# Hybrid decoder step: every third key unit multiplied on GpSimd instead of VectorE

## The chip, the cores and the metric

The kernel runs on one core of a Trainium2 chip, as one launch. Times are device microseconds. The engines are TensorE (PE, matrix products), VectorE (DVE), ScalarE (ACT), GpSimd (POOL) and SyncE (SP, which here only issues transfers). Each engine works through its own list of instructions in order; semaphores tie the lists together. What is measured is the time of one execution, as the median of several; less is better.

## The reference, cut to what matters

One inference step of a two-layer decoder trunk runs for a prompt of 1024 tokens and for 8 single new tokens (samples). The first layer has two groups of heads side by side: stick-breaking attention and an RWKV-7 recurrence. Each sample attends with 8 heads of 64 columns over 8192 old keys and values, which lie in pages of 128 tokens, 64 pages a sample, in an order given by a page table. The part that this change touches is the scores of the samples against the old keys:

```python
z = einsum('bthd,bshd->bhts', q, past_k) * DH_A ** -0.5 + bias      # one query row a sample
w = sb_weights(z, ...)                                             # sums over later positions
o = einsum('bhts,bshd->bthd', w, past_v)
```

The recurrence of the prompt, which runs at the same time in the kernel, is computed in 8 pairs of chunks of 64 tokens, each pair by gram matrices, a triangular solve in five levels, and an update of the state.

## The kernel before, in words

The kernel is a row of phases with a barrier between them. Sample work on pages is spread over four of them (the projections of values and of RWKV inputs, the prompt's attention, and the recurrent stage `rwkv_phase`) by a class `Pages`, whose methods add instructions to the list of each engine at the places where the phases call them.

A key unit is two key pages: 128 tokens on the partitions, 2 x 512 columns. There are 256 units, 32 a sample. SyncE loads the pages into a ring of 8 pages, that is 4 units (`load_keys`, L1018 reads the page number, L1019 issues the transfer), each after the semaphore `k_used` says that its slot is free. `keys_dve` handles a unit on VectorE in two instructions: L1108 multiplies the two pages by the query row, which has been copied to all partitions, into a buffer `prod`, and then frees the slots; L1111 sums groups of 64 columns of `prod` into 16 scores. The units 0 to 81 are done before the recurrent stage, by VectorE, and stay there.

In the recurrent stage a loop over `i` makes eight turns. VectorE's list of a turn is the recurrence of pair `i`, with `more(n)` between its steps, which puts `n` key units of sample `i + 1` there: 3, 2, 1, 2, 2, 1, 2, 2, 2, 2 and at the end 6, 25 in all. (The last turn has none; it puts the steps of the sample state there.) In this document the units of a turn are counted 0 to 24. After the last one `bias_dve` (L1125) adds the bias, and ScalarE (L1077 to L1079) and VectorE (L1130) start on the softplus of that sample at the head of the next turn. L2120, L2127, L2140 and L2143 are the masked copies of the solve; the first `L2033` with `rw_dh` is the update of the state, which waits for TensorE.

GpSimd issues the transfers of the value pages, which are weighted and added by TensorE (L1048, four pages a group, twelve groups of the current sample and four of the one before in a turn). The ring of value pages has 12 slots, so page `at` waits until page `at - 12` has been used; the page number is read into a register first (`load_values`, L1070). Before the first page of each sample GpSimd issues the next pair's input rows (`rows`, L1481), which ScalarE reads (L1811) in the next turn. Pages of a sample are counted 0 to 63 here; a sample's pages 0 to 47 are used in its own turn, 48 to 63 in the next.

Before the stage GpSimd clears small buffers (L1483 to L1485); nothing else of its work is arithmetic.

Of the kernel before, what the change touches and what calls it, by code (L numbers as in the profile page):

```python
# [17 lines left out]
ALU = mybir.AluOpType  # L18
ACT = mybir.ActivationFunctionType
AX = mybir.AxisListType  # L20

P = 128
D_MODEL = 1024
SEQ = 1024
NS = 8
# [4 lines left out]
H_A, DH = 8, 64  # L30
D_A = H_A * DH
PAST, PAGE = 8192, 128
NPG = PAST // PAGE
# [10 lines left out]
NPAIR = SEQ // (2 * C)  # L44
# [65 lines left out]
class Sems:  # L110


    def __init__(self, nc, phase):
        self.nc, self.phase, self.all = nc, phase, []
# [841 lines left out]
class Pages:  # L956
# [3 lines left out]
    RING = 8  # L960
    VRING = 12
    ZRING = 4
    UNITS = NPG // 2

    def __init__(self, T, ctx):
        nc = T.nc
        self.T, self.nc = T, nc
        self.sems = sems = Sems(nc, "pages")
        self.k_in = [sems(f"k_in{n}") for n in range(self.RING)]
        self.v_in = [sems(f"v_in{n}") for n in range(self.VRING)]  # L970
        (self.qc_in, self.q_turned, self.q_copied, self.q_stored, self.q_in, self.table_in, self.k_used, self.v_used,
         self.reduced, self.biased, self.logged, self.softplus_ready, self.summed, self.z_ready, self.w_ready,
         self.cleared, self.folded, self.selected, self.picked, self.step, self.act_step) = (
            sems(n) for n in ("qc_in", "q_turned", "q_copied", "q_stored", "q_in", "table_in", "k_used", "v_used",
                              "reduced", "biased", "logged", "softplus_ready", "summed", "z_ready", "w_ready",
                              "fold_cleared", "folded", "selected", "picked", "page_step", "page_act_step"))
        sb = lambda n, s, d=F32: ctx.enter_context(nc.sbuf_tensor("pg" + n, s, d))
        self.kp = sb("_k", [P, self.RING, D_A])
        self.qc, self.q = sb("_qc", [P, 4, NS]), sb("_q", [P, 2, D_A])
        self.fold = sb("_fold", [P, D_A])  # L980
        self.qr = self.fold[0:NS, :]
        self.prod = sb("_prod", [P, 2, D_A])
        self.z = sb("_z", [P, self.ZRING, H_A, NPG])
        self.zb, self.sp = sb("_zb", [P, H_A * NPG]), sb("_sp", [P, H_A * NPG])
        self.wts = sb("_w", [P, 2, H_A * NPG])
        self.table = sb("_table", [1, NS * NPG], I32)
        self.q_rows = nc.dram_tensor("scratch_pg_q", [NS, D_A], F32, kind="Internal").ap()
        self.fetched, self.unit = 0, 0
# [71 lines left out]
    def start_act(self, act):  # L1060
        act.wait_ge(self.cleared, 1)
        act.wait_ge(self.q_turned, 1)
        act.activation(self.qr, self.T.ps[0:NS, 7, :], ACT.Copy, scale=DH ** -0.5).then_inc(self.q_copied, 1)

    def load_values(self, pool, pages):

        for at in pages:
            pool.wait_ge(self.v_used, at + 1)
            page = pool.value_load(self.table[0:1, at:at + 1], min_val=0, max_val=self.T.n_phys - 1)
            pool.dma_start(self.vp[:, at % self.VRING, :], self.T.io["v_pages"][bass.ds(page, 1), :, :]  # L1070
                           .rearrange("a p n -> (a p) n")).then_inc(self.v_in[at % self.VRING], 16)
# [27 lines left out]
    def keys_dve(self, dve, n):  # L1099

        for u in range(self.unit, min(self.unit + n, NS * self.UNITS)):
            b, g, at = u // self.UNITS, 2 * u % NPG, 2 * u % self.RING
            if g == 0:
                dve.wait_ge(self.q_in, 16 * b + 16)
            for e in range(2):
                dve.wait_ge(self.k_in[at + e], 16 * (2 * u // self.RING) + 16)
            dve.wait_ge(self.reduced, u + 1)
            dve.tensor_tensor(self.prod[:, :, :], self.kp[:, at:at + 2, :],  # L1108
                              self.q[:, b % 2, :].unsqueeze(1).to_broadcast([P, 2, D_A]), ALU.mult).then_inc(self.k_used, 2)
            dve.wait_ge(self.k_used, self.RING + 2 * u + 2)  # L1110
            dve.tensor_reduce(self.z[:, b % self.ZRING, :, g:g + 2].rearrange("p h n -> p n h"),  # L1111
                              self.prod[:, :, :].rearrange("p n (h d) -> p n h d", h=H_A), AX.X, ALU.add)\
               .then_inc(self.reduced, 1)
            self.unit = u + 1

# [4 lines left out]
    def bias_dve(self, dve, b):  # L1120
        assert self.unit >= self.UNITS * (b + 1)
        dve.wait_ge(self.reduced, self.UNITS * (b + 1) + 1)
        if b:
            dve.wait_ge(self.w_ready, b)
        dve.tensor_tensor(self.zb[:, :].rearrange("p (h n) -> p h n", h=H_A), self.z[:, b % self.ZRING, :, :],  # L1125
                          self.T.vec("sb_bias").unsqueeze(2).to_broadcast([P, H_A, NPG]), ALU.add).then_inc(self.biased, 1)
# [14 lines left out]


KEYS_V, KEYS_PB, KEYS_ATT, KEYS_TURN = 16, 42, 24, 25


def attention_phase(T):
# [239 lines left out]
def rwkv_phase(T):  # L1386
# [6 lines left out]
    nc, h, ps, io = T.nc, T.h, T.ps, T.io  # L1393
    sems = Sems(nc, "rwkv")
# [14 lines left out]
    pages = T.pages  # L1409
    with ExitStack() as ctx:  # L1410
# [23 lines left out]
        u, r0 = ur[:, 0, :], ur[:, 1, :]  # L1434
# [25 lines left out]
        def _(sp):  # L1460
            pages.load_keys(sp, NS * Pages.UNITS)
            sp.wait_ge(pages.k_used, Pages.RING + NS * NPG)
# [13 lines left out]
        @block.gpsimd  # L1476
        def _(pool):
            def rows(i):
                pool.wait_ge(S["turned"], i)
                pool.wait_ge(S["bonus_used"], prep(i - 1) + 1)  # L1480
                pool.dma_start(X[:, :, :], xs[:, :, i * W:(i + 1) * W]).then_inc(xs_in, 16)  # L1481

            pool.memset(main["eg"][:, :, :], 1.0)  # L1483
            pool.memset(smpl["eg"][:, :, :], 1.0)
            pool.memset(Hx[:, :, :, :], 0.0).then_inc(S["cleared"], 1)  # L1485
            pool.wait_ge(S["cleared"], 1)
            pool.sem_inc(S["h_ready"], 1)
            done = Pages.VRING
            for i in range(1, NPAIR):
                rows(i)  # L1490
                pages.load_values(pool, range(done, NPG * i))
                done = NPG * i
            pages.load_values(pool, range(done, NPG * NS))

        @block.tensor
        def _(pe):
# [1705 lines left out]
```

## Time and profile before

| | us |
|---|---|
| timed runs, median of 3 (lowest to highest) | 4689.95 (4687.75 to 4692.08) |
| profiled execution, its own time | 4680.17 |
| its span, first to last instruction | 4678.6 |
| TensorE busy in the span | 3857.8 |
| VectorE busy | 2356.5 |
| ScalarE busy | 1174.9 |
| GpSimd busy | 401.3 |
| key units on VectorE, multiplies (L1108, 256 times) | 313.5 |
| key units on VectorE, sums (L1111, 256 times) | 312.9 |
| value page issues on GpSimd (L1070, 512 times) | 276.3 |

The recurrent stage lies at about 694 to 1540 us of the span. A busy time is the time in which an engine had an instruction at work; waits on semaphores, register work and the issuing of transfers by SyncE are not counted. In the rows further down, "start us, us" is when an instruction or a merged row of them began and how long it took; "x2" counts them; a bracket gives the idle time of the engine just before and what ended it. "<-issue" is idle time for which the profile shows no other engine.

### The profile page before, as it was taken

The numbers are of one execution on the slowest core, as the hardware profiler recorded it, in microseconds if no ns is written. First come the engines' busy times: TensorE is split into PE (matmuls) and PEld (weight loads), VectorE is DVE, ScalarE is ACT, GpSimd is POOL, SyncE is SP. The second block draws the span as 40 slices with busy tenths as digits, with TensorE's granted clock in tenths as the row PEclk, the third lists the DMA queues.
The fourth block names the chain that finished last, engine by engine and source line by source line (L and its number), as shares of the span: only waits on it lengthen the run. The fifth ranks groups of instructions, "written<-read, shape, count | busy, mean of one in ns | idle before, by whom it ended". The sixth has DMA issues, their size and how long they took to land. (4 is left out here: it accounts for less than half of the span.)

```text
span 4678.6 us, 77751 instructions
## 1 busy us (share of the span) xinstructions
PE 3857.8 (82%) x29645; PEld 3332.9 (71%) x29645; DVE 2356.5 (50%) x3054; ACT 1174.9 (25%) x1872; POOL 401.3 (9%) x739
## 2 busy tenths in 40 slices
PE   6887885676677769999896999788898187999999
PEld 5786333344444659999896888677777087999899
DVE  2488888888887224444312444444443524444511
ACT  3213662222222222222212222222221012222300
POOL 0011102333333100000000000000000000000000
PEclk8998997788888689999998999877777598999999
DMA  2465316988887321111122222210100231111122
GB/s 89 152 209 167 114 48 213 309 290 290 288 289 246 106 113 46 45 46 45 60 73 105 70 86 83 82 33 19 37 19 15 76 133 52 51 45 46 44 82 64
DMA packets 212106, 512.43 MB, mean 110 GB/s; under 512 B 34153, under 2 KB 67321, under 8 KB 205298
## 3 DMA queue, kind: packets, MB, share of 16 engines
q1 hardware_dynamic: 148306, 305.03, 20.2%
q0 software_dynamic: 62640, 203.84, 12.6%
q8 instruction: 152, 2.49, 0.2%
q14 instruction: 96, 0.79, 0.1%
q10 hardware_dynamic: 912, 0.28, 0.0%
HBM read 454.87 MB, written 54.56 MB: 109 GB/s over the span
## 5 line engine op out<-in xcount | busy, mean ns | idle before, releaser
L263 PE MATMUL ps<-ffn_hh,up_wh 128*128 128x344 f32 x2112 | 678.5, 321 | 60.3 <-DVE up_wl L255 60.3
L265 PE MATMUL ps<-ffn_hl,up_wh 128*128 128x344 f32 x2112 | 676.8, 320 | 0.0
L264 PE MATMUL ps<-ffn_hh,up_wl 128*128 128x344 f32 x2112 | 676.0, 320 | 0.0
L263 PEld LDWEIGHTS ps<-ffn_hh,up_wh 128*128 128x128 f32 x2112 | 398.6, 189 | 61.4 <-issue 61.4
L264 PEld LDWEIGHTS ps<-ffn_hh,up_wl 128*128 128x128 f32 x2112 | 398.7, 189 | 0.0
L265 PEld LDWEIGHTS ps<-ffn_hl,up_wh 128*128 128x128 f32 x2112 | 398.6, 189 | 0.0
L458 PE MATMUL ps<-down_ah,down_wh 128*128 128x344 f32 x1056 | 342.0, 324 | 30.7 <-DVE down_al L492 18.2
L459 PE MATMUL ps<-down_ah,down_wl 128*128 128x344 f32 x1056 | 338.7, 321 | 0.0
L460 PE MATMUL ps<-down_al,down_wh 128*128 128x344 f32 x1056 | 338.7, 321 | 0.0
L1108 DVE TENSOR_TENSOR pg_prod<-pg_k,pg_q 128x1024 f32<-128x1024 f32 x256 | 313.5, 1225 | 35.3 <-DVE rw_mxt L2143 4.6
L1070 POOL DMA_DIRECT2D pg_v<-in_v_pages x512 | 276.3, 540 | 558.9 <-issue 508.5
L1111 DVE TENSOR_REDUCE pg_z<-pg_prod 128x16 f32<-128x1024 f32 x256 | 312.9, 1222 | 8.8
L263 PE MATMUL ps<-hh,odd_wh 128*128 128x344 f32 x792 | 258.3, 326 | 66.1 <-DVE odd_wl L255 66.1
L264 PE MATMUL ps<-hh,odd_wl 128*128 128x344 f32 x792 | 254.5, 321 | 0.0
L265 PE MATMUL ps<-hl,odd_wh 128*128 128x344 f32 x792 | 254.4, 321 | 0.0
L458 PEld LDWEIGHTS ps<-down_ah,down_wh 128*128 128x128 f32 x1056 | 199.6, 189 | 35.3 <-issue 29.4
L1048 PE MATMUL ps<-pg_v,pg_w 128*8 128x512 f32 x1024 | 165.0, 721 | 57.7 <-DMA pg_v<-in_v_pages 57.6
L263 PEld LDWEIGHTS ps<-hh,odd_wh 128*128 128x128 f32 x792 | 150.2, 190 | 75.0 <-ACT odd_row L2362 44.9
L459 PEld LDWEIGHTS ps<-down_ah,down_wl 128*128 128x128 f32 x1056 | 200.6, 190 | 0.0
L460 PEld LDWEIGHTS ps<-down_al,down_wh 128*128 128x128 f32 x1056 | 199.7, 189 | 0.0
L255 DVE TENSOR_TENSOR down_wl<-down_w,down_wh 128x896 fp32r<-128x896 f32 (+1 forms) x48 | 54.4, 1137 | 280.3 <-ACT down_wh L250 280.3
L663 DVE TENSOR_TENSOR ffn_a<-up_cv,ps 128x344 f32 (+1 forms) x132 | 67.4, 510 | 245.4 <-PE ps L265 245.4
(457 smaller groups left out, 7318.4 us busy)
## 6 DMA issues: line engine op xcount, KB each, us to landing
pg_k<-in_k_pages SPq DMA_DIRECT2D x512, 256.0 KB, 4.4
pg_v<-in_v_pages POOLq DMA_DIRECT2D x512, 256.0 KB, 4.7
up_w<-in_w_ff SPq DMA_DIRECT2D x44, 1034.0 KB, 4.8
odd_w<-in_w_odd SPq DMA_DIRECT2D x33, 526.0 KB, 4.0
scratch_odd_rows<-odd_cv POOLq DMA_DIRECT2D x32, 516.0 KB, 4.6
down_w<-in_w_down SPq DMA_DIRECT2D x32, 448.0 KB, 3.4
dn_x<-scratch_odd_rows SPq DMA_DIRECT2D x8, 1536.0 KB, 7.8
scratch_x<-out_x POOLq DMA_DIRECT2D x16, 516.0 KB, 2.9
```

What stands on the lines that cost most here:

```text
L255: dve.tensor_tensor(lo, w, hi.bitcast(F32), ALU.subtract).then_inc(rest_ready, 1)
L263: pe.matmul(out, wh, xh, start=(k == 0), stop=False)
L264: pe.matmul(out, wl, xh, start=False, stop=False)
L265: mm = pe.matmul(out, wh, xl, start=False, stop=(k == n - 1))
L458: pe.matmul(out, hi, ah[:, k, g[c]], start=(k == 0), stop=False)
L459: pe.matmul(out, lo, ah[:, k, g[c]], start=False, stop=False)
L460: mm = pe.matmul(out, hi, al[k][:, g[c]], start=False, stop=(k == FT - 1))
L663: dve.tensor_tensor(a[:, bass.ds(2 * i + j, 1), col].rearrange("p a t -> p (a t)"), cv[:, j, col], ps[:, 3 + c, 0:GC], ALU.mult).then_inc( ...
L1048: pe.matmul(self.T.ps[c:c + H_A, 7, :], wts[:, :, g], self.vp[:, (NPG * b + g) % self.VRING, :], start=(g < 4), stop=(g >= NPG - 4), tile_ ...
L1070: pool.dma_start(self.vp[:, at % self.VRING, :], self.T.io["v_pages"][bass.ds(page, 1), :, :] .rearrange("a p n -> (a p) n")).then_inc(sel ...
L1108: dve.tensor_tensor(self.prod[:, :, :], self.kp[:, at:at + 2, :], self.q[:, b % 2, :].unsqueeze(1).to_broadcast([P, 2, D_A]), ALU.mult).th ...
L1111: dve.tensor_reduce(self.z[:, b % self.ZRING, :, g:g + 2].rearrange("p h n -> p n h"), self.prod[:, :, :].rearrange("p n (h d) -> p n h d" ...
```

## The change

The units 84, 87, 90, ... 255, 58 of the 174 units of the recurrent stage, are multiplied by GpSimd. The product is written over the keys in the ring, and VectorE sums it there (`prod` is not used); the slots are freed after this sum. A semaphore `multiplied` tells VectorE that the product is there, and VectorE waits for its own sum before it frees the slots. GpSimd waits for the query row and for the two key pages. Its loop over the value pages now goes in steps of four; ahead of each four it issues the products of all units up to a bound that runs with the page number, 10 units on from the share of the turn that the pages have reached. The input rows (`rows`) are issued ahead of the same pages as before, and ahead of the products at that place.

```diff
+    FIRST = 84
...
+    def on_pool(self, u):
+        return u >= self.FIRST and (u - self.FIRST) % 3 == 0
+
+    def keys_pool(self, pool, u):
+        b, at = u // self.UNITS, 2 * u % self.RING
+        pool.wait_ge(self.q_in, 16 * b + 16)
+        for e in range(2):
+            pool.wait_ge(self.k_in[at + e], 16 * (2 * u // self.RING) + 16)
+        pool.tensor_tensor(self.kp[:, at:at + 2, :], self.kp[:, at:at + 2, :],
+                           self.q[:, b % 2, :].unsqueeze(1).to_broadcast([P, 2, D_A]), ALU.mult).then_inc(self.multiplied, 1)
...
+            z = self.z[:, b % self.ZRING, :, g:g + 2].rearrange("p h n -> p n h")
+            if self.on_pool(u):
+                dve.wait_ge(self.multiplied, (u - self.FIRST) // 3 + 1)
+                dve.tensor_reduce(z, self.kp[:, at:at + 2, :].rearrange("p n (h d) -> p n h d", h=H_A), AX.X, ALU.add)\
+                   .then_inc(self.reduced, 1)
+                dve.wait_ge(self.reduced, u + 2)
+                dve.sem_inc(self.k_used, 2)
+                self.unit = u + 1
+                continue
...
 KEYS_V, KEYS_PB, KEYS_ATT, KEYS_TURN = 16, 42, 24, 25
+KEYS = KEYS_V + KEYS_PB + KEYS_ATT
...
-            done = Pages.VRING
-            for i in range(1, NPAIR):
-                rows(i)
-                pages.load_values(pool, range(done, NPG * i))
-                done = NPG * i
-            pages.load_values(pool, range(done, NPG * NS))
+            unit = Pages.FIRST
+            for at in range(Pages.VRING, NPG * NS, 4):
+                if at == Pages.VRING or at % NPG == 0 and at < NPG * (NPAIR - 1):
+                    rows(at // NPG + 1)
+                while unit < min(KEYS + KEYS_TURN * (at - Pages.VRING) // NPG + 10, NS * Pages.UNITS):
+                    pages.keys_pool(pool, unit)
+                    unit += 3
+                pages.load_values(pool, range(at, at + 4))
```

## Rows read from the trace of the kernel before

**Rows 1.** Stretches, one a turn: us, busy time (instructions) by engine, clock, DMA share, GB/s.

```profile
core 0: us, PE busy (x) PEld busy (x) DVE busy (x) ACT busy (x) POOL busy (x), PEclk, DMA share, GB/s
819.50:925.10 105.60, 71.73 (x952) 43.66 (x952) 92.69 (x102) 25.67 (x48) 37.56 (x69) 0.82 0.90 306
...
1030.80:1136.80 106.00, 70.90 (x952) 42.66 (x952) 92.68 (x102) 25.62 (x48) 35.60 (x65) 0.84 0.90 297
...
1242.50:1348.40 105.90, 72.50 (x952) 43.89 (x952) 92.68 (x102) 25.66 (x48) 35.62 (x65) 0.82 0.86 296
```

**Rows 2.** VectorE's groups in the turn 1030.8 to 1136.8: busy us, mean ns, idle before.

```profile
L1111 DVE TENSOR_REDUCE pg_z<-pg_prod 128x16 f32<-128x1024 f32 x26 | 31.8, 1222 | 0.9
L1108 DVE TENSOR_TENSOR pg_prod<-pg_k,pg_q 128x1024 f32<-128x1024 f32 x25 | 30.7, 1227 | 4.7 <-DVE rw_mxt L2143 0.6 <-DMA pg_k<-in_k_pages 0.6 <-DVE rw_mrb L2033 0.4
...
L2033 DVE TENSOR_TENSOR rw_dh<-rw_Hx,ps 64x256 f32<-64x256 f32 x4 | 1.7, 417 | 3.4 <-PE ps L1648 3.3
...
L1130 DVE SCALAR_TENSOR_TENSOR pg_sp<-pg_zb,pg_sp 128x512 f32<-128x512 f32 x1 | 0.7, 692 | 2.0 <-ACT pg_sp L1079 2.0
```

**Rows 3.** GpSimd in order of time in that turn: pages 16, 20, 52 and 63.

```profile
1078.41 0.54 POOL L1070 DMA_DIRECT2D pg_v<-in_v_pages  x1 [2.43 <-issue]
...
1083.03 0.54 POOL L1070 DMA_DIRECT2D pg_v<-in_v_pages  x1 [0.62 <-issue]
...
1122.23 0.54 POOL L1070 DMA_DIRECT2D pg_v<-in_v_pages  x1 [0.62 <-issue]
...
1134.95 0.54 POOL L1070 DMA_DIRECT2D pg_v<-in_v_pages  x1 [0.61 <-issue]
```

**Rows 4.** VectorE in order of time, units 19, 20 and 24 of that turn.

```profile
1121.30 1.23 DVE L1108 TENSOR_TENSOR pg_prod<-pg_k,pg_q 128x1024 f32<-128x1024 f32 x1 [0.33 <-DVE h L2033]
1122.56 1.22 DVE L1111 TENSOR_REDUCE pg_z<-pg_prod 128x16 f32<-128x1024 f32 x1
1123.92 1.22 DVE L1108 TENSOR_TENSOR pg_prod<-pg_k,pg_q 128x1024 f32<-128x1024 f32 x1
...
1134.37 1.23 DVE L1108 TENSOR_TENSOR pg_prod<-pg_k,pg_q 128x1024 f32<-128x1024 f32 x1
```

**Rows 5.** VectorE in order of time, the state update and units 10 and 11.

```profile
1076.29 0.87 DVE L2033 TENSOR_TENSOR rw_dh<-rw_Hx,ps 64x256 f32<-64x256 f32 x2 [3.34 <-PE ps L1648]
...
1078.38 1.23 DVE L1108 TENSOR_TENSOR pg_prod<-pg_k,pg_q 128x1024 f32<-128x1024 f32 x1 [0.31 <-DVE rw_Hx L2033]
...
1083.26 1.25 DVE L1108 TENSOR_TENSOR pg_prod<-pg_k,pg_q 128x1024 f32<-128x1024 f32 x1
```

**Rows 6.** GpSimd's groups of the whole span, its largest clearing.

```profile
L2495 POOL MEMSET dn_S<- 128x1024 f32 x1 | 1.0, 952 | 20.6 <-POOLq L124 20.6
```

**Rows 7.** GpSimd in order of time before the stage, the first value pages.

```profile
559.93 0.54 POOL L1189 DMA_DIRECT2D at_q<-out_qk_rows  x1 [63.78 <-PE ps L1243]
...
563.52 1.10 POOL L1198 DMA_DIRECT2D rw_xsmp<-scratch_xs_rows  x1
564.61 1.11 POOL L1070 DMA_DIRECT2D pg_v<-in_v_pages  x2
565.96 0.54 POOL L1070 DMA_DIRECT2D pg_v<-in_v_pages  x1 [0.24 <-issue]
567.11 0.54 POOL L1070 DMA_DIRECT2D pg_v<-in_v_pages  x1 [0.61 <-issue]
```

**Rows 8.** TensorE and ScalarE in order of time, turn's head and last value groups.

```profile
1031.48 0.63 ACT L1077 ACTIVATE pg_sp<-pg_zb 128x512 f32<-128x512 f32 x1 [25.89 <-DVE pg_zb L1125]
1035.98 1.98 PE L1565 MATMUL ps<-rw_AR,rw_e 64*64 64x128 f32 x32 [11.91 <-ACT rw_mvtm L1873]
...
1116.54 1.91 PE L1048 MATMUL ps<-pg_v,pg_w 128*8 128x512 f32 x8 [2.46 <-DMA pg_v<-in_v_pages]
1121.35 1.91 PE L1048 MATMUL ps<-pg_v,pg_w 128*8 128x512 f32 x8 [2.90 <-DMA pg_v<-in_v_pages]
```

**Rows 9.** Next input rows: their issue and reading in time, and their landing.

```profile
1029.51 1.10 POOL L1481 DMA_DIRECT2D rw_xs<-scratch_xs_rows  x1
1051.04 0.30 ACT L1811 ACTIVATE rw_eg<-rw_xs 64x128 f32<-64x128 f32 x1
...
DMA to landing us min/median/max: 6.8/10.1/10.3
```

**Rows 10.** Line L1019, the key page transfers, over four turns from 925 to 1348.

```profile
L1019 SPq DMA_DIRECT2D pg_k<-in_k_pages x200: 332/333/666, 925.7 to 1347.9; - x100
...
DMA to landing us min/median/max: 2.5/5.0/10.7
```

More of the change, by code:

```diff
@@ L970, in __init__ @@
         self.v_in = [sems(f"v_in{n}") for n in range(self.VRING)]
-        (self.qc_in, self.q_turned, self.q_copied, self.q_stored, self.q_in, self.table_in, self.k_used, self.v_used,
+        (self.qc_in, self.q_turned, self.q_copied, self.q_stored, self.q_in, self.table_in, self.k_used, self.v_used, self.multiplied,
          self.reduced, self.biased, self.logged, self.softplus_ready, self.summed, self.z_ready, self.w_ready,
          self.cleared, self.folded, self.selected, self.picked, self.step, self.act_step) = (
-            sems(n) for n in ("qc_in", "q_turned", "q_copied", "q_stored", "q_in", "table_in", "k_used", "v_used",
+            sems(n) for n in ("qc_in", "q_turned", "q_copied", "q_stored", "q_in", "table_in", "k_used", "v_used", "multiplied",
                               "reduced", "biased", "logged", "softplus_ready", "summed", "z_ready", "w_ready",
@@ L1110, in keys_dve @@
             dve.wait_ge(self.k_used, self.RING + 2 * u + 2)
-            dve.tensor_reduce(self.z[:, b % self.ZRING, :, g:g + 2].rearrange("p h n -> p n h"),
-                              self.prod[:, :, :].rearrange("p n (h d) -> p n h d", h=H_A), AX.X, ALU.add)\
+            dve.tensor_reduce(z, self.prod[:, :, :].rearrange("p n (h d) -> p n h d", h=H_A), AX.X, ALU.add)\
                .then_inc(self.reduced, 1)
```

## The prediction, made before the changed kernel ran

> **What bounds the kernel now.** I read the table of stretches first, cut at the eight times at which VectorE adds the page bias (L1125), which closes one turn of the recurrent stage and opens the next. A full turn takes 105.6 to 106.0 us, and VectorE is busy in 92.7 of them, TensorE in about 72, GpSimd in about 36; the DMA share is 0.86 to 0.90 [rows 1]. Then VectorE's groups in one turn, the fourth: 25 key units cost 30.7 us of multiplies (L1108) and 31.8 of sums (L1111), two thirds of its busy time, and its only longer waits are 3.3 us for TensorE before L2033 and 2.0 us for ScalarE before L1130 [rows 2]. The rest of the 106 us is the small gap behind each instruction. So VectorE's order of work sets the turn. Last, GpSimd's order in time: it issues the value pages 1.155 us apart (0.54 busy, 0.61 between), and from page 16 of a turn to page 63 almost without a break, 1078.41 to 1134.95 [rows 3]. It is no idle engine in that half of the turn.
>
> **The change part by part.** Of the 174 units of this stage, 58 (84, 87, ..., 255) lose their VectorE multiply, 8 or 9 a turn, 8.33 on average.
>
> Removed from VectorE: a unit repeats after 2.62 us where units follow each other (1121.30 to 1123.92), and its sum with the gap behind it takes 1.36 (1122.56 to 1123.92) [rows 4]. That leaves 1.26 us, of which I give 0.06 to the added wait for the unit's own sum and the semaphore step: 1.2 us a unit, 8.33 x 1.2 = 10.0 us a turn. The ends: 1.26 if the step is free, 1.0 if it costs a gap of 0.3 as before L1108 at 1078.38 [rows 5].
>
> Not all of it shortens the turn. Units 8 and 9 of a turn stand ahead of the 3.34 us wait for TensorE at 1076.29 [rows 5]; TensorE's work there hangs on an earlier VectorE step, so what these two units save becomes more of that wait. One of them is a GpSimd unit in two turns of three: 0.67 x 1.2 = 0.8 us a turn back.
>
> Added wait: VectorE now waits for the product, with everything behind it queued. GpSimd issues unit k of a turn at a fixed page: units 11 and 12 behind page 19, units 14 and 15 behind page 27. Page 20 went out at 1083.03, and VectorE took unit 11 at 1083.26 [rows 3, 5]. There is no lead: a product begun at 1082.6 and taking 1.9 us (below) is ready at 1084.5, 1.3 us late; by the same count unit 14 is 0.4 late in that turn, unit 16 0.9 in another, none in the third: mean 0.9 us a turn. Ends 0 and 8.33 x 1.9 = 15.8, if every product began only when VectorE was there.
>
> The price of the product. No row shows GpSimd doing arithmetic on two tensors. Its nearest row is the clearing of as many elements, 128x1024 in 0.95 us, which writes one stream [rows 6]; a product reads two and writes one, so 0.95 is the lower end and three such passes, 2.86, the upper. VectorE's 1.23 for the same multiply lies between. I take two passes, 1.9 us, the two reads one after the other and the write beside them.
>
> GpSimd's queue: what counts is how much later the pages behind a product go out. When GpSimd was busy with other issues from 559.93 on, the next two pages followed back to back, the third after 0.24, and only then came the steady 0.61 [rows 7]: the preparation of a page runs beside the engine's work, and about 0.61 + 0.61 + 0.37 = 1.6 us of it can be hidden. A product of 1.9 us thus delays the pages by 0.3; with 0.2 for its three waits, h = 0.5 us. Ends: 0 and 2.86 + 0.2 = 3.1, if nothing overlaps. Three things cover h. First, the last products of a turn: unit 24 is issued ahead of page 52, which went out at 1122.23, and VectorE took it at 1134.37 [rows 3, 4]: 12.1 us of lead, of which five products take 2.5. Second, TensorE already waits 2.46 and 2.90 us for late value pages; later pages make it later, but at the turn's head it idles 11.91 us for ScalarE, which itself waited 25.89 us for the bias [rows 8]. Third, the next input rows (L1481) went out at 1029.51 behind the last page and land in 10.1 us, and ScalarE read them at 1051.04 [rows 9]: 11.4 us to spare, less 6.7 x 0.5. With these covers gone, each further us of h would cost five a turn.
>
> What VectorE loses while GpSimd multiplies. If the two cannot read their second operands at once, a VectorE multiply that comes due during a product waits for its end. Typically the product starts as a VectorE multiply ends; then a sum of 1.36 us with one operand follows, and the next multiply waits 1.9 - 1.36 = 0.54 us: 8.33 x 0.54 = 4.5 us a turn. Ends: 0, and 2.86 - 1.36 = 1.5 a product, 12.5 a turn. I take 4.5, which goes with the 1.9.
>
> [...]
>
> The early release of a key slot moves from the multiply's end to the sum's end in these units. Keys land 5.0 us (median, 10.7 at most) after their issue [rows 10], against some 8 us for four units with two GpSimd ones among them; with the product behind it this is tight in the last six units, and I count it with the added wait's upper end. SP issues the same pages, in the same order; L1481's place in the order is kept.
>
> Sum for a turn: -10.0 + 0.8 + 0.9 + 4.5 = -3.8 us. Turns 1 to 6 count in full; turn 0 begins late behind its own preparation and turn 7 has no units, so I put both at nothing. 6 x 3.8 = 23 us. The profiled execution took 4680.2 (span 4678.6), 10 us under the median of the timed runs, so the difference is taken off the median: 4689.95 - 23 = 4667.
>
> **The rivals.**
>
> *A, reads do not collide.* VectorE keeps all but 1.7 us: -8.3 a turn, -50, 4640. For it: nothing in the trace shows contention. [...] The DMA share of 0.90 in a turn allows a turn of 97.
>
> *B, the gain is eaten.* A product of 2.3 us lies between the 1.9 I take and the 2.86 of its upper end; its loss is 0.94, 7.8 a turn, and the turn gains 0.5: -3, 4687. For it: the loss grows with the whole excess of the product over 1.36, and from 2.4 us on it takes all of the 8.3. Against it: a product may start beside two one-operand instructions in a row, and then costs nothing. [...]
>
> *C, GpSimd's queue becomes the bound (slower).* Place: pages 12 to 51, already without slack, and the product of unit 24 behind them. Price: 5 h against 12.1 us of lead, so the turn is longer from h = 2.4 on. That needs a product that hides no preparation, since its wait for keys stops the sequencer as well, with keys landing late. At h = 3.0: +2.9 a turn, +17, 4707. A product of 2.86 us with its full loss of 12.5 comes to +4.2 a turn, +25, 4715, and I count it here. Against: the pages that followed back to back [rows 7].
>
> That the products are not made on GpSimd, or fewer than 58, cannot be: the list of units is fixed.
>
> **How the numbers follow.** The forecast, a partial gain (own range 4655 to 4680), has 0.30; A 0.19, B 0.26, C 0.25. A difference under 0.2%, 9.4 us, is no change for this kernel. Faster: 0.27 of the forecast, A, and 0.04 of B: 0.50. Same: 0.03 of the forecast, 0.19 of B, 0.02 of C: 0.24. Slower: the rest of B and C, 0.26. The range takes in A with a little more gain and C at h = 3: 4632 to 4708.
>
> **What would show it.** In the table of stretches a turn near 102 us, with VectorE busy 10 us less. The products should last near 1.9 us. VectorE's multiplies just after a product's start should be longer or start late by some 0.5 us; if none does, A; if by 0.9 or more, B. VectorE's waits for GpSimd should sum to about 1 us a turn; several us, growing to the turn's end, with pages issued over 1.5 us apart on average, is C. The prediction is wrong if the turn stays at 105 or more, or falls below 99.

## The result and the profile after

The changed kernel takes 4699.34 us in the median of 20 runs (4690.18 to 4713.70), the kernel before 4687.03 in 20 runs of the same study (4675.01 to 4693.74): a ratio of 1.0033 [1.0025, 1.0040]. It is slower by 0.3%, where 4667 was forecast. In the ratios of this document one execution of 12593 us, of e13 below, far off all others of its kernel, is left out.

The profiled execution of after happened to be its slowest, 4713.70 us (span 4712.2), and that of before, 4680.17, lies 7 under its median. So not all of the 33.5 us between the two profiles is the change. The stage begins 8.8 us later in the trace of after (first bias at 702.96, against 694.16), and some 7.5 us more lie behind the stage; no work differs there, and I take both for differences between executions. Inside the stage turn 0 takes 130.3 us (before 125.3), turns 1 to 6 together 639.5 (before 632.0), and turn 7 to the stage's end 4.7 more. What follows goes by turns 1 to 6, "the six turns", cut in every kernel at the bias instructions as [rows 1] were.

The table of stretches of before, the six turns in one row: us, then the busy time of PE, PEld, DVE, ACT, POOL (instructions), granted TensorE clock, DMA share, GB/s.

```profile
819.50:1451.50 632.00, 432.85 (x5712) 262.47 (x5712) 553.81 (x599) 153.92 (x288) 214.27 (x392) 0.83 0.87 295
```

The same of after, and three of its turns, which answer to [rows 1]:

```profile
833.30:1472.80 639.50, 449.12 (x5712) 272.90 (x5712) 545.46 (x550) 153.25 (x288) 332.37 (x438) 0.80 0.85 290
...
833.30:937.10 103.80, 75.80 (x960) 45.82 (x960) 88.87 (x94) 25.58 (x48) 55.75 (x75) 0.81 0.90 311
...
1044.80:1153.40 108.60, 72.81 (x944) 45.72 (x944) 94.50 (x92) 25.66 (x48) 54.63 (x74) 0.80 0.82 280
...
1257.90:1364.70 106.80, 74.97 (x952) 46.43 (x952) 87.92 (x93) 25.35 (x48) 56.38 (x73) 0.80 0.84 289
```

VectorE lost 50 multiplies of 1.226 us (61 us; the count falls by only 49, since one more bias instruction is counted at the window's end), but its busy time fell by only 8.3 us. The rest of the 61 us is in instructions that became longer. VectorE's groups of after in the six turns (busy us, mean ns, idle before them and its releasers):

```profile
L1130 DVE TENSOR_TENSOR pg_prod<-pg_k,pg_q 128x1024 f32<-128x1024 f32 x99 | 140.7, 1422 | 24.3 <-DVE pg_z L1121 8.4 <-DVE rw_mxt L2167 2.6 <-DMA pg_k<-in_k_pages 2.5
L1133 DVE TENSOR_REDUCE pg_z<-pg_prod 128x16 f32<-128x1024 f32 x100 | 122.3, 1223 | 3.4
L1121 DVE TENSOR_REDUCE pg_z<-pg_k 128x16 f32<-128x1024 f32 x50 | 60.8, 1216 | 14.3 <-POOL pg_k L1075 12.5 <-DVE rw_Hx L2057 0.2
...
L2057 DVE TENSOR_TENSOR rw_Hx<-rw_dh,rw_eend 64x256 f32<-64x256 f32 x24 | 13.4, 556 | 0.8
L2087 DVE TENSOR_SCALAR rw_e<-rw_e 128x1024 f32<-128x1024 f32 x6 | 12.8, 2139 | 0.9
L2106 DVE SCALAR_TENSOR_TENSOR rw_K<-rw_K,rw_xs 128x512 f32<-128x512 f32 x6 | 10.9, 1817 | 0.2
L2057 DVE TENSOR_TENSOR rw_dh<-rw_Hx,ps 64x256 f32<-64x256 f32 x24 | 10.0, 418 | 21.5 <-PE ps L1672 20.9
```

The rows of before for three of these groups, in the same six turns:

```profile
L2033 DVE TENSOR_TENSOR rw_Hx<-rw_dh,rw_eend 64x256 f32<-64x256 f32 x24 | 10.1, 420 | 0.8
...
L2063 DVE TENSOR_SCALAR rw_e<-rw_e 128x1024 f32<-128x1024 f32 x6 | 4.2, 694 | 0.9
...
L2082 DVE SCALAR_TENSOR_TENSOR rw_K<-rw_K,rw_xs 128x512 f32<-128x512 f32 x6 | 4.2, 692 | 0.2
```

The multiplies that VectorE kept grew from 1226 to 1422 ns, other instructions with two operands in SBUF up to 2.6 times (rw_K, 692 to 1817), a tensor_scalar, which has one, threefold (694 to 2139), while the sums (1223, 1216) and instructions with one operand in PSUM (rw_dh, 416, now 418; rw_makr, 1214, now 1218, with three of its six begun during a product) kept their length. GpSimd's products and page issues in the six turns:

```profile
L1083 POOL DMA_DIRECT2D pg_v<-in_v_pages x382 | 207.9, 545 | 241.7 <-issue 229.8 <-PE ps L1049 9.1 <-DMA pg_k<-in_k_pages 1.8
L1075 POOL TENSOR_TENSOR pg_k<-pg_k,pg_q 128x1024 f32<-128x1024 f32 x50 | 120.9, 2418 | 65.4 <-DMA pg_k<-in_k_pages 64.9
```

A product takes 2.42 us, not 1.9, and GpSimd waits 65 us for keys with pages queued behind. TensorE's wait for value pages in the six turns (total us, times, longest), in before:

```profile
PE ps L1048 <- DMA pg_v<-in_v_pages: 39.0, 17, 4.2
```

and in after:

```profile
PE ps L1049 <- DMA pg_v<-in_v_pages: 72.0, 22, 9.1
```

TensorE's matmuls also take longer, 449.1 us against 432.9, at a mean granted clock of 0.80 against 0.83. Neither reached VectorE in these turns: its wait for TensorE before rw_dh is 20.9 us, against 20.2.

How one product meets VectorE is seen in the order of time (start, us, and in brackets the idle time before it). GpSimd in after:

```profile
1105.14 0.54 POOL L1083 DMA_DIRECT2D pg_v<-in_v_pages  x1 [0.62 <-issue]
1105.69 2.39 POOL L1075 TENSOR_TENSOR pg_k<-pg_k,pg_q 128x1024 f32<-128x1024 f32 x1
...
1117.69 2.41 POOL L1075 TENSOR_TENSOR pg_k<-pg_k,pg_q 128x1024 f32<-128x1024 f32 x1
...
1128.45 0.54 POOL L1083 DMA_DIRECT2D pg_v<-in_v_pages  x1 [0.62 <-DMA pg_k<-in_k_pages]
1129.00 2.37 POOL L1075 TENSOR_TENSOR pg_k<-pg_k,pg_q 128x1024 f32<-128x1024 f32 x1
1131.30 1.64 POOL L1083 DMA_DIRECT2D pg_v<-in_v_pages  x3
1133.20 0.54 POOL L1083 DMA_DIRECT2D pg_v<-in_v_pages  x1 [0.26 <-issue]
1144.94 2.33 POOL L1075 TENSOR_TENSOR pg_k<-pg_k,pg_q 128x1024 f32<-128x1024 f32 x1 [11.20 <-DMA pg_k<-in_k_pages]
```

VectorE at the same times:

```profile
1099.18 1.21 DVE L1121 TENSOR_REDUCE pg_z<-pg_k 128x16 f32<-128x1024 f32 x1
1100.72 1.23 DVE L1130 TENSOR_TENSOR pg_prod<-pg_k,pg_q 128x1024 f32<-128x1024 f32 x1 [0.33 <-DVE pg_z L1121]
...
1106.22 2.98 DVE L1130 TENSOR_TENSOR pg_prod<-pg_k,pg_q 128x1024 f32<-128x1024 f32 x1 [0.33 <-DVE rw_on L2185]
...
1118.66 2.00 DVE L2104 SCALAR_TENSOR_TENSOR rw_K<-rw_e,vecs_sb 128x512 f32<-128x512 f32 x1
...
1129.05 2.88 DVE L2057 TENSOR_TENSOR rw_kk<-rw_kk,rw_ksq 128x512 f32<-128x512 f32 x1
```

The product of 1105.69 ends at 1108.08. VectorE's multiply, begun at 1106.22 in its midst, ends at 1109.20, 1.12 us after the product, which is nearly its whole usual length. The two others behave alike: 1118.66 ends 0.56 after the product of 1117.69, 1129.05 ends 0.56 after that of 1129.00, at a usual length of 0.69. All eleven multiplies that begin during a product in the six turns end 1.07 to 1.12 us after it and are counted as 1.62 to 2.98 us long: the wait is part of their busy time, and nearly their whole usual length, 1.23, comes after the product.

The bracket at 1100.72 is the wait for the sum's own end, 0.33 us. The pages around 1129.00 show how little a product delays GpSimd's queue when its keys are there and the pages behind it have their slots: from 1128.45 to 1133.20 is four page steps in 4.75 us, where four steps take 4.62 without one [rows 3]. Behind the product of 1105.69 the next page goes out 3.90 us after the last one; it probably waited for its slot, since TensorE ended a value group only at 1107.86, 1.18 us before that page.

### The profile page after: what moved, and what is told of

The parts are those of the page before. It is cut to its first block and busy times, and to the rows that moved or that the text cites. A ratio compares the mean times of both kernels' runs of the same rounds, so it can differ in the third digit from the quotient of the medians.

```text
span 4712.2 us, 77755 instructions
## 1 busy us (share of the span) xinstructions
PE 3900.5 (83%) x29645; PEld 3360.5 (71%) x29645; DVE 2348.1 (50%) x2996; ACT 1173.4 (25%) x1872; POOL 540.7 (11%) x797
## 3 DMA queue, kind: packets, MB, share of 16 engines
q8 instruction: 152, 2.49, 0.2%
## 5 line engine op out<-in xcount | busy, mean ns | idle before, releaser
L1130 DVE TENSOR_TENSOR pg_prod<-pg_k,pg_q 128x1024 f32<-128x1024 f32 x198 | 266.9, 1348 | 33.4 <-DVE pg_z L1121 10.0
L1133 DVE TENSOR_REDUCE pg_z<-pg_prod 128x16 f32<-128x1024 f32 x198 | 242.1, 1223 | 6.8
```

Of the source, the lines that this page charges most:

```text
L1133: dve.tensor_reduce(z, self.prod[:, :, :].rearrange("p n (h d) -> p n h d", h=H_A), AX.X, ALU.add)\
```

## The experiments

Theory 1: VectorE loses time because its instructions with two SBUF operands stand still while GpSimd reads. Theory 2: GpSimd's queue is held up by its products and their waits, and value pages go out late. One table first; the reading follows by group. Six turns in us; "rest" is the time less VectorE's busy time; the last column is TensorE's wait for value pages (39.0 before). The ratio is of timed runs, the rest of one profile each: e4 and e8 are equal in the timed runs and 6.5 us apart in their six turns, so differences of that size in the columns decide nothing.

| kernel | ratio to before, 95% | six turns | VectorE busy | rest | PE for pages |
|---|---|---|---|---|---|
| before | 1 | 632.0 | 553.8 | 78.2 | 39.0 |
| after | 1.0033 [1.0025, 1.0040] | 639.5 | 545.5 | 94.0 | 72.0 |
| e1 reads beside | 1.0149 [1.0135, 1.0163] | 686.9 | 610.0 | 76.9 | 40.6 |
| e6 one clearing beside | 1.0045 [1.0031, 1.0058] | 644.0 | 567.3 | 76.7 | 45.0 |
| e2 three clearings beside | 1.0080 [1.0067, 1.0093] | 664.6 | 555.0 | 109.6 | 100.1 |
| e4 signal only | 0.9915 [0.9899, 0.9931] | 594.4 | 492.3 | 102.1 | 80.6 |
| e8 signal, no key waits | 0.9918 [0.9905, 0.9932] | 600.9 | 492.6 | 108.3 | 61.0 |
| e7 one clearing for the product | 0.9965 [0.9951, 0.9978] | 609.6 | 499.4 | 110.2 | 71.8 |
| e3 three clearings for it | 1.0073 [1.0057, 1.0089] | 661.8 | 495.3 | 166.5 | 115.4 |
| e5 product without keys | 1.0046 [1.0032, 1.0059] | 645.1 | 547.8 | 97.3 | 46.4 |
| e9 pairs, started | 1.0134 [1.0119, 1.0150] | 694.3 | 487.0 | 207.3 | 19.5 |
| e10 pairs alone | 1.0124 [1.0107, 1.0142] | 691.9 | 486.1 | 205.8 | 18.6 |
| e11 pairs, signal only | 0.9967 [0.9955, 0.9979] | 617.1 | 485.9 | 131.2 | 49.0 |
| e12 placed earlier | 1.0027 [1.0016, 1.0038] | 646.0 | 486.5 | 159.5 | 110.9 |
| e13 four in gaps | 0.9991 [0.9980, 1.0003] | 630.7 | 514.4 | 116.3 | 50.3 |

**Work on GpSimd beside the kernel before (e1, e6, e2).** VectorE keeps all its multiplies, and GpSimd does something useless at the 58 places of the changed kernel. Its results go to columns of `h` that nothing reads until later. In the diffs of this section, which are shortened, DEAD stands for these columns and SCAN for a block of constants. Each such instruction also waits for the end of the one before it, and VectorE's last turn for all 58.

```diff
+        pool.tensor_tensor(DEAD, SCAN, SCAN, ALU.mult)                # e1: reads and writes
+        pool.memset(DEAD as uint8 [:, :, 0:660], 0)                   # e6: only writes
+        pool.memset(DEAD, 0.0)                                        # e2: only writes, three pieces,
+        pool.wait_ge(self.paced, n + 1)                               #     each waits for the one before
+        ...
```

> The kernel before, unchanged on VectorE, with 58 products of 128x1024 added to GpSimd's list at the places of the change, from constants into columns that nobody reads, with no wait for keys and nobody waiting for them. Theory 1 (VectorE's two-operand reads and GpSimd's reads shut each other out): VectorE's multiplies and its other instructions with two SBUF operands grow by about 1 us a product, 55 to 60 us in all, one-operand sums and PSUM reads stay as they are, and as VectorE sets the turn the time rises by 40 to 60 us, to about 4730 to 4745. Theory 2 (it is GpSimd's queue, held up by waits for keys): VectorE's durations stay, and the time rises by less than 10 us, since no wait for keys is there.

> As e1, but GpSimd clears columns at those places instead (three clearings one after the other, 0.95 + 0.95 + 0.31 us and two waits, about 2.4 us): the same time on GpSimd, no reading. Theory 1: no VectorE instruction grows, and the time is that of before within 10 us, 4680 to 4697. Theory 2 in its plain form, that 2.4 us at the head of the queue are enough to make the value pages late: 10 to 20 us slower than before, with TensorE's wait for value pages up.

> As e2, but one clearing of 2640 one-byte elements a row in place of three with waits between them, so that GpSimd's list is stopped by nothing but the engine's own 2 us or so: writes only, no keys. Theory 1 (only reads shut VectorE out) and theory 2 (only waits that stop GpSimd's list make pages late) agree here: VectorE's durations stay, the preparation of pages runs on beside the clearing, and the time is within 10 us of before, against +36 in e2. If it is again 20 us or more slower, the mere length of an operation in the list makes the pages late, and e2's waits were not the reason.

e1: 1.98 us of reading and writing on GpSimd, with no tie to VectorE before the last turn, makes the kernel 1.5% slower. VectorE's busy time in the six turns rises by 56 us, 1.12 for each of 50 products, and the rest doesn't change (76.9): the whole loss is VectorE's. The standstill goes both ways: the shortest of these products lasts 1.90 us, the longest 2.76, and one that begins 0.48 us into a VectorE multiply (at 1091.35) 2.49. e6 is the control: its clearing is longer, 2.32 us, and two-operand instructions are untouched. Two groups of VectorE in e1, a multiply and the tensor_scalar:

```profile
L1117 DVE TENSOR_TENSOR pg_prod<-pg_k,pg_q 128x1024 f32<-128x1024 f32 x149 | 213.2, 1431 | 25.3 <-DVE rw_mxt L2155 3.9 <-DVE rw_mrb L2045 2.5 <-DVE rw_kk L2045 2.0
...
L2075 DVE TENSOR_SCALAR rw_e<-rw_e 128x1024 f32<-128x1024 f32 x6 | 11.0, 1832 | 0.9
```

The same in e6, and the two other groups that became clearly longer there, a small copy and a smaller tensor_scalar:

```profile
L1116 DVE TENSOR_TENSOR pg_prod<-pg_k,pg_q 128x1024 f32<-128x1024 f32 x149 | 182.8, 1227 | 25.3 <-DVE rw_mxt L2154 3.9 <-DVE rw_mrb L2044 2.5 <-DVE h L2044 2.0
...
L2074 DVE TENSOR_SCALAR rw_e<-rw_e 128x1024 f32<-128x1024 f32 x6 | 10.5, 1754 | 0.9
...
L2117 DVE COPY rw_eend<-rw_eL 128x8 f32<-128x8 f32 x6 | 6.1, 1014 | 0.0
...
L2049 DVE TENSOR_SCALAR rw_eg<-rw_eg 128x256 f32<-128x256 f32 x6 | 3.6, 593 | 0.9
```

In before the first tensor_scalar took 694 ns (above); the other two groups:

```profile
L2038 DVE TENSOR_SCALAR rw_eg<-rw_eg 128x256 f32<-128x256 f32 x6 | 1.8, 295 | 0.9
...
L2106 DVE COPY rw_eend<-rw_eL 128x8 f32<-128x8 f32 x6 | 1.0, 167 | 0.0
```

So there are two groups of victims. Instructions with two operands in SBUF lost to the GpSimd instruction that reads (the multiply, 1226 to 1431 ns), not to the one that only writes (1227). A tensor_scalar lost to either (694 to 1832 and to 1754), and the copy to the writing one (167 to 1014; in e1 its six took 162, and none of them began during a product). The means hide that it is all or nothing: of e6's six tensor_scalars on rw_e the three that met a clearing took 2.61 to 2.92 us, which is nearly the clearing and their own length (2.32 and 0.69), and the three others 0.69. The three groups account for 13.2 of e6's 13.5 us ((1754 - 694) x 6, (1014 - 167) x 6 and (593 - 295) x 6), and e6's slowdown of 12.0 us in the six turns, which its expectation did not foresee, is that and no queue: TensorE's wait for value pages is 45.0, near before's 39.0.

e2 had been meant as the control, and failed as one: TensorE waits 100 us for pages, while VectorE's busy time (555.0) stays. Behind e2's clearings the next page never goes out in under 0.83 us, behind e6's it follows at once in 35 of 49 cases; I read this as inner waits that stop the preparation of pages. The two runs differ in the clearing's type too, so the cause isn't wholly isolated. e2 is 36 us slower than before, where the single instruction of e6, as long in all, held up next to nothing.

**The product taken out of the changed kernel (e4, e8, e7, e3, e5).** The products are left out in all five; GpSimd signals instead (e4, e8), clears dead columns (e7 once, e3 in three pieces with waits), or multiplies constants (e5). In e8 and e5 GpSimd waits for no keys; VectorE does.

```diff
-        pool.tensor_tensor(self.kp[:, at:at + 2, :], self.kp[:, at:at + 2, :], ..., ALU.mult).then_inc(self.multiplied, 1)
+        pool.sem_inc(self.multiplied, 1)                              # e4, e8
+        pool.memset(DEAD as uint8, 0).then_inc(self.multiplied, 1)    # e7
+        pool.tensor_tensor(DEAD, SCAN, SCAN, ALU.mult).then_inc(self.multiplied, 1)   # e5
-        pool.wait_ge(self.k_in[at + e], ...)                          # e8, e5: VectorE waits for the keys instead
```

> The changed kernel, but GpSimd only waits for the query and the keys and signals; the 58 products are left out of the result. Theory 1: a few us under e3, 4625 to 4650. Theory 2: GpSimd still stands at the waits for keys, so that the value pages are late: above 4680. If e4 lies far under e3, the product's own length in the queue counts and not the wait in front of it.

> The changed kernel without products and without key waits on GpSimd, which only signals; VectorE waits for the keys itself. The 58 products are left out of the result. This is what taking the multiplies off VectorE is worth by itself: 50 to 65 us under before, 4620 to 4635, with turns near 97 us. Against e4 (38 under before, turns of 99.1 us) it shows what the key waits at the head of GpSimd's list cost: theory 1 expects at most 10 us of difference, theory 2 twenty or more.

> The changed kernel with all its waits, with one such clearing (writes only) in the place of the product; the 58 products are left out of the result. Theory 1: VectorE's two-operand instructions are back at their durations of before, the sums come as early as with the product, and the time is 20 to 38 us under before (e4, with nothing in that place, was 38 under), that is 35 to 50 under the changed kernel. Theory 2: within 10 us of the changed kernel, since its key waits are all there.

> The changed kernel with all its waits, but GpSimd clears unused columns (about 2.4 us) in the place of the product, and then signals; the 58 products are left out of the result. Theory 1: the waits for keys stay, the reads are gone; VectorE keeps what it saved, and the time falls by 35 to 60 us under the kernel before, to 4630 to 4655. Theory 2: the waits for keys and the late value pages stay, so the time stays within 10 us of the changed kernel, 4690 to 4710.

> The changed kernel, but GpSimd multiplies constants into unused columns and does not wait for keys; VectorE waits for the keys of these units itself and for the signal. The products of keys are left out of the result. Theory 1: VectorE's instructions still grow by about 1.1 us a product, and the time stays within 10 us of the changed kernel or falls by what late pages cost, to no less than before - 10, 4673. Theory 2: GpSimd no longer stands for keys (86 us in the changed kernel), the pages come in time, and the time falls by 30 us or more, under 4670.

e4 and e8 give the upper limit of the idea: a product that costs nothing. VectorE's busy time falls by 61, the time of the six turns by 38 and 31, and the timed runs by 38 and 37 us; for e8 50 to 65 had been expected. e4 keeps the key waits on GpSimd, e8 has none, and they are equal in the timed runs (0.9915, 0.9918); e5, which takes the key waits from GpSimd but keeps an instruction that reads, is no better than after (1.0046 and 1.0033). The 65 us that GpSimd idles for keys are thus not what the changed kernel loses. Theory 2 in that form is out, but for a few us of the last turn (below).

What takes half of the 61 us is seen in VectorE's waits for others in e8 (total us, times, longest):

```profile
DVE rw_dh L2055 <- PE ps L1670: 24.2, 9, 5.2
DVE pg_prod L1128 <- DMA pg_k<-in_k_pages: 13.1, 14, 2.2
...
DVE rw_mxt L2165 <- PE ps L1609: 7.9, 5, 2.5
DVE pg_prod L1128 <- DVE pg_z L1119: 7.1, 22, 0.3
DVE pg_z L1119 <- DMA pg_k<-in_k_pages: 6.0, 6, 1.5
```

In before VectorE waited 1.0 us for key pages; here 19.1. It waits 32.1 for TensorE (before 20.2) and 7.1 for its own sums. The next limits lie close behind VectorE; whether the keys come late by their ring of eight pages or by the transfers' rate wasn't tried.

e7 differs from after by one thing, a GpSimd instruction of 2.31 us that reads nothing in the place of one of 2.42 that reads. It is 0.35% faster than before, after 0.33% slower. VectorE's busy time is 46 us less than after's. e5 reads constants, not keys, and VectorE's busy time is back at 547.8. The reading costs the changed kernel about 0.7%, more than its slowdown. e7 itself lies 0.5% above e4, which has nothing in that place, and gains 15 us where 20 to 38 were expected: there VectorE waits 19.5 us for the clearings, and 7 us more are in longer instructions. So the way from the upper limit (0.9915) to after (1.0033) is some 0.5% for the length of the instruction and 0.7% for its reading. e3 repeats e2's lesson (TensorE 115.4 us for pages).

**Products that begin under the sums (e9, e10, e11).** If the reading is the loss, a product should lie beside the sums, which kept their length beside it (1223 and 1216 ns in after). VectorE takes units in threes: two multiplies (the second into the dead columns), then two sums, then the sum of the product. e9 lets GpSimd begin when the second multiply has ended; e10 lets it begin by itself; e11 is e9 with the products left out. 56 units, eight a turn, are GpSimd's, and `more(n)` is cut into threes.

```diff
+        pool.wait_ge(self.k_used, self.RING + 2 * u)                  # e9, e11: second multiply done
+PRODUCTS = (2, 0), (5, 3), (8, 12), (11, 12), (14, 23), (17, 36), (20, 53), (23, 58)   # unit, before which page
+            held = [u, u + 1] if pair ... else [u]                    # both multiplies, then both sums
```

> All results complete. VectorE now takes its units in threes: two multiplies, then three sums, the third of GpSimd's product; GpSimd begins that product only when the second multiply has ended, and 56 of 174 units are GpSimd's. Theory 1 (the loss is VectorE's multiplies and other two-operand instructions standing still while GpSimd reads): a product of 2.43 us now lies beside two sums with their gaps, 2 x 1.36 = 2.7 us, and collides with nothing but what a late start leaves over; VectorE's lengthening in turns 1 to 6 falls from 53 us to under 12, and the time to 10 to 38 us under before (ratio 0.992 to 0.998). Theory 2 (the loss is in GpSimd's queue, whose value pages go out late behind the products): GpSimd now also waits for VectorE with pages queued behind it, so the pages go out later still and the time is at or above that of the changed kernel, 12 to 40 us over before (1.003 to 1.009).

> The same order of units on VectorE and the same places in GpSimd's order, but GpSimd doesn't wait for VectorE's second multiply: a product begins as soon as its keys are there. All results complete. Theory 1: a product begins at any point of VectorE's work and meets two-operand instructions again; the two multiplies in a row are hit less often than two single ones, so VectorE's lengthening is 15 to 40 us in turns 1 to 6, and the time lies between the run with the start and the changed kernel, -15 to +10 us. Theory 2: better than the run with the start by the time that GpSimd no longer waits, 5 to 20 us.

> As the run with the start, every wait kept, but GpSimd gives only its signal where the product was: the products of 56 units are left out. It is the floor for that order of units. Both theories: 30 to 45 us under before (0.990 to 0.994), if the new order costs VectorE nothing by itself; with 20 or less, the order of units costs something of its own. The run with the start stands above it by what the products still cost.

On the time both theories' numbers failed: theory 1 expected a gain, and e9 loses 1.3%, more than theory 2 allowed. On the mechanism theory 1 held. VectorE's groups in e9:

```profile
L1142 DVE TENSOR_TENSOR pg_prod<-pg_k,pg_q 128x1024 f32<-128x1024 f32 x53 | 64.9, 1225 | 18.5 <-DMA pg_k<-in_k_pages 6.6 <-DVE rw_mrb L2083 2.6 <-DVE pg_z L1127 2.5
L1145 DVE TENSOR_TENSOR h<-pg_k,pg_q 128x1024 f32<-128x1024 f32 x48 | 58.7, 1223 | 0.0
L1127 DVE TENSOR_REDUCE pg_z<-pg_k 128x16 f32<-128x1024 f32 x48 | 58.6, 1222 | 126.2 <-POOL pg_k L1077 126.2
```

The multiplies are back at 1225 and 1223 ns and VectorE's busy time (487.0) stands at that of e11 (485.9), in which GpSimd multiplies nothing: the lengthening is gone. But VectorE now waits 126 us for products, 2.6 each, so that more than half of the products' 113 us lies beside a VectorE that stands still. That the sums don't suffer is better seen in e12 below, where, added up from the order of time, some 83 of the products' 113 us lie under sums, their mean is 1212 to 1222 ns, and the busy time is 486.5. e10 shows the same waits, so the start signal is not to blame; its 15 to 40 us of lengthening didn't come, since its products, too, were late. TensorE hardly waits for pages (19.5), so late pages are not to blame either. e11 is a warning of its own: without products this order gains 15 us (0.9967), not the 30 to 45 expected. VectorE waits 40.6 us there for the bare signal, and 19.1 for keys, so the order of units and the places in GpSimd's list cost about half of the upper limit.

Why the products of e9 come late is seen in two of one turn, GpSimd first:

```profile
1097.68 2.35 POOL L1077 TENSOR_TENSOR pg_k<-pg_k,pg_q 128x1024 f32<-128x1024 f32 x1
1107.16 2.36 POOL L1077 TENSOR_TENSOR pg_k<-pg_k,pg_q 128x1024 f32<-128x1024 f32 x1 [7.14 <-DVE h L1145]
```

and VectorE:

```profile
1089.71 1.22 DVE L1145 TENSOR_TENSOR h<-pg_k,pg_q 128x1024 f32<-128x1024 f32 x1
...
1100.06 1.22 DVE L1127 TENSOR_REDUCE pg_z<-pg_k 128x16 f32<-128x1024 f32 x1 [6.88 <-POOL pg_k L1077]
...
1105.83 1.25 DVE L1145 TENSOR_TENSOR h<-pg_k,pg_q 128x1024 f32<-128x1024 f32 x1
...
1109.55 1.22 DVE L1127 TENSOR_REDUCE pg_z<-pg_k 128x16 f32<-128x1024 f32 x1 [0.21 <-POOL pg_k L1077]
```

Where GpSimd stood waiting (1107.16), the product lay under the sums and VectorE waited 0.21 us. Where it stood behind pages that themselves waited for a slot (1097.68, seven us after the multiply's end at 1090.93), VectorE waited 6.88. The products stood too late among the pages.

**The same with other places, and with fewer products (e12, e13).**

```diff
-PRODUCTS = (2, 0), (5, 3), (8, 12), (11, 12), (14, 23), (17, 36), (20, 53), (23, 58)
+PRODUCTS = (2, 0), (5, 1), (8, 8), (11, 12), (14, 20), (17, 29), (20, 46), (23, 51)    # e12
+PRODUCTS = (2, 0), (5, 1), (8, 8), (11, 12)                                            # e13, 28 products in all
```

> All results complete. As the run in which GpSimd begins a product at VectorE's second multiply, but GpSimd's products stand earlier among its pages (before pages 0, 1, 8, 12, 20, 29, 46, 51 of a turn, in the place of 0, 3, 12, 12, 23, 36, 53, 58), so that GpSimd mostly stands ready when VectorE comes. In that run VectorE's lengthening was gone, but it waited 126 us in turns 1 to 6 for products that began late. If only their places were late, VectorE's wait for GpSimd falls to 20 to 60 us and the time to 10 to 40 us under before (0.991 to 0.998). If a product held for VectorE costs as much through the pages behind it, TensorE's wait for value pages grows from 19.5 us to over 80 and the time stays 20 us or more over before (1.004 or more).

> All results complete. As the run with earlier places, but only the first four products of a turn (28 in all) are GpSimd's: they stand where GpSimd in the kernel before lies idle, 14 us at a turn's head and 10 us behind page 11, and the page stream from page 16 to 63 is left alone. VectorE saves 24 multiplies of 1.22 us in turns 1 to 6, 29 us, and waits some 5 to 15 us for products: 10 to 28 us under before (0.994 to 0.998). If it comes out better than eight products with earlier places, the page stream is what limits the number of products; if worse, VectorE's multiplies still are.

e12 falls between its two cases. The longest waits in its six turns, of VectorE:

```profile
DVE pg_z L1127 <- POOL pg_k L1077: 51.0, 48, 5.1
DVE rw_mxt L2193 <- PE ps L1637: 48.0, 11, 8.7
```

and of TensorE:

```profile
PE ps L1049 <- DMA pg_v<-in_v_pages: 110.9, 33, 13.1
```

VectorE's wait for products fell from 126 to 51, as the places had promised, and 48 us better in the six turns came of it (694.3 to 646.0). But GpSimd, ready ahead of time, holds back the pages behind it (its own wait for VectorE's multiply is 107 us), TensorE waits 110.9 us for them, and VectorE 48.0 us for TensorE at rw_mxt. Early places cost pages, late places cost VectorE. e13 keeps only products in GpSimd's idle stretches; it is level with before, 0.9991 [0.9980, 1.0003], where 0.994 to 0.998 was expected, with 20.6 us of waits for products and 29.9 at rw_mxt against 29 us of multiplies. The 29.9 are not pages alone: in e11, without products, this order of units already waits 11.1 us there, and in e13 TensorE's matmuls take 458 us at a granted clock of 0.78 (433 at 0.83 in before). Which of these weighs most is open. No version with real products beat the kernel before.

## Why the prediction was wrong

**The failed step** is "What VectorE loses while GpSimd multiplies". I forecast 4.5 us a turn, 0.54 a product. With e8 as the kernel without products, VectorE's instructions grew by 545.5 - 492.6 = 52.9 us in the six turns: 8.8 a turn, 1.06 for each of 50 products. The mechanism was the forecast's as far as a multiply waits for the product's end; that it is the second operands that collide no run shows. The size that I gave it was half. One cause is the price of the product, 2.42 us where I took 1.9. My formula with the measured price gives 2.42 - 1.36 = 1.06, which fits too well: e1 and e5, whose products last 1.98 and 1.94, lose 1.12 and (547.8 - 492.6) / 50 = 1.10 each, where it gives 0.6. What failed in it is that a product starts as a VectorE multiply ends. It starts anywhere, and costs about half of its length (0.44 of it here, 0.57 in e1 and e5); and the victims are not the key multiplies alone (1226 to 1422 ns), but also instructions of the stage with two operands in SBUF that meet a product (rw_K, 692 to 1817, rw_Hx, 420 to 556), and the tensor_scalar, which has one (694 to 2139).

**The sum with measured terms**, a turn: removed 61.2 / 6 = -10.2 (forecast -10.0); lengthened +8.8 (+4.5); wait for products 12.5 / 6 = +2.1 (+0.9); wait for the own sum 8.4 / 6 = +1.4 (I gave it 0.06 a unit, 0.5 a turn; each step costs 0.33 where a multiply follows). That is +2.1; the turns measure +1.25. The wait for the own sum is gross: many multiplies that now follow such a sum had waited as long behind another instruction, and the idle time before VectorE's multiplies is 24.3 us in after, 26.0 in before. The 0.8 in front of TensorE didn't come: that wait is 20.9 us in the six turns, 20.2 before.

**Turn 0** I put at nothing; it takes 5.0 us more in the trace. VectorE waits 5.98 us there for one product, ahead of this sum:

```profile
773.25 1.22 DVE L1121 TENSOR_REDUCE pg_z<-pg_k 128x16 f32<-128x1024 f32 x1 [5.98 <-POOL pg_k L1075]
```

**Turn 7** I put at nothing, too. To TensorE's first matmul of the state update it takes 97.4 us, 92.7 in before. GpSimd still has 76 value pages to issue when this turn begins, 66 in before, and TensorE waits 21.0 us for them, 14.4 in before. e7 and e4, which keep GpSimd's waits for keys, have 77 and 78 pages left and take 95.7 and 95.0 us; e5 and e8, without these waits, 66 and 71 pages and 91.7 and 92.1 us. So the late queue probably costs the changed kernel these few us here, where VectorE has no units left; one profile of each kernel shows it, and no run isolates it.

**The rivals.** A is out by e1. B named the point, "from 2.4 us on it takes all of the 8.3", and ended at no change; with the waits the outcome lies 12 us above it. C is out as the main cause: where its keys and the slots are there a product delays the pages by 0.13 us (I took h = 0.5), and e6 shows hardly later pages. The pages of after are later, behind the waits for keys (72.0 against 39.0 us of waiting on TensorE), but as far as the traces show that cost time in turn 7 alone. C's side, slower, came out for another reason; of what I counted there, VectorE's full loss of 12.5 us a turn is nearest to the 8.8 measured.

**What I had not asked** is what the removed work is worth by itself. I took the 8.3 us a turn of rival A as free to have; e8 shows 31 us in the six turns, 5.2 a turn, since VectorE then waits for keys and for TensorE. With that limit the forecast's gain would have been a fraction of its 23 us at most, even at its own price of the collision: 5.2 less 4.5 and 0.9 a turn leaves nothing.

## What to carry to other kernels

Work moved from VectorE to GpSimd was not wholly removed here: of the 61.2 us that VectorE loses without the products (e8), 52.9 came back in after as longer instructions. Count VectorE's instructions with two SBUF operands (the multiply, 1226 to 1422 ns) and its tensor_scalar (694 to 2139), beside clearings also its small copies (167 to 1014, e6), that run in the meantime; in a list like this one about half of the GpSimd instruction's length was lost for each one moved (0.44 of it in after, 0.57 in e1 and e5). Ask what is late next before counting a gain: 61 us less VectorE work was worth 31 to 38 here. In this queue, which also issues transfers, 2.32 us of work without waits cost the transfers little (e6, 45.0 us of waiting for pages against 39.0), but waits in it held the transfers behind them (e2, 100.1; e12, 110.9), and moving the product only traded that wait for one of VectorE (e9, 19.5 us for pages and 126 for products; e12, 110.9 and 51.0).

## What was not expected of the hardware

The clearing of e6, which reads nothing, stretched a VectorE tensor_scalar from 694 to 1754 ns and a copy of 8 columns from 167 to 1014 in the mean (up to 2.92 and 2.73 us), and left a two-operand multiply at 1227. GpSimd's preparation of pages ran on beside a product in after: the three pages behind that of 1129.00 followed back to back, and the fourth was 0.13 us late. A product of keys in place, with the query row repeated for the second page, took 2.36 to 2.42 us in the mean (e9, after; 2.33 at the least), one of two constant blocks of the same size 1.94 to 1.98 (e5, e1; 1.89 at the least); which of the differences makes it wasn't tried.
